# Gate and value projections of two layers as seven block products, with two of a panel's four weight sums on GpSimd

## What is computed

```python
def swiglu(u, w1, w3, w2):
    return (jax.nn.silu(u @ w1) * (u @ w3)) @ w2

for l in range(DEPTH):                                   # DEPTH = 2
    ada = (c_act @ w_ada[l] + b_ada[l])[:, None, :]
    sh1, sc1, g1, sh2, sc2, g2 = jnp.split(ada, 6, axis=-1)
    u = h * (1.0 + sc1) + sh1
    y = mixer(u, ...)
    h = layer_norm(DN_ALPHA * h + g1 * y, ln1_g[l], ln1_b[l])
    u = h * (1.0 + sc2) + sh2
    y = swiglu(u, w1[l], w3[l], w2[l])
    h = layer_norm(DN_ALPHA * h + g2 * y, ln2_g[l], ln2_b[l])
```

## Time and profile before

| | us |
|---|---|
| median of 3 runs | 2424.16 |
| lowest and highest run | 2416.7 and 2425.68 |
| the profiled execution | 2416.46 |
| its span, first to last instruction | 2414.7 |

### The profile page before, as it was taken

The page is one execution under the profiler, slowest core; times in us unless marked ns, Lnnn a source line. Parts: engine busy times, 40 slices in busy tenths (PEclk is TensorE's granted clock), DMA queues, the critical chain, the costliest instruction groups (busy, mean ns, idle before and its releaser), DMA issues.

```text
span 2414.7 us, 27153 instructions
## 1 busy us (share of the span) xinstructions
PE 2324.4 (96%) x10982; PEld 1835.2 (76%) x10982; DVE 1253.5 (52%) x2360; ACT 494.2 (20%) x1048; POOL 62.6 (3%) x93
## 2 busy tenths in 40 slices
PE   7999999999999999999999999999999999888998
PEld 5888587788768876868887655588888874567987
DVE  5764311432746432125777266775566455556666
ACT  1222320100011223101011355312200032432200
POOL 0100000000000000000000000000000000000000
PEclk9999999999999999999999999999999999999999
DMA  9853433674475333336874101433333245134442
GB/s 392 321 210 106 156 122 126 233 289 166 175 283 196 134 110 145 124 136 249 305 288 166 35 36 36 148 113 134 121 123 140 79 141 187 74 113 170 161 158 79
DMA packets 163499, 391.18 MB, mean 162 GB/s; under 512 B 6448, under 2 KB 10928, under 8 KB 160560
## 3 DMA queue, kind: packets, MB, share of 16 engines
q1 hardware_dynamic: 136736, 285.03, 32.7%
q0 software_dynamic: 24080, 93.69, 10.6%
q10 hardware_dynamic: 2560, 10.72, 1.2%
HBM read 388.37 MB, written 1.05 MB: 161 GB/s over the span
## 4 chain that ended last, share of the span: by engine, by line
PE 91%; DVE 4%; ACT 2%; DMA 1%; issue 1%; DVEq 0%; SPq 0%; ACTq 0%
PE bank L503 89%; DVE arena L1946 2%; PE bank L501 2%; ACT arena L1335 2%; DVE arena L1952 1%; DMA arena<-in_w_ada 1%; ACT arena L1338 1%; DVE arena L1949 0%; DMA arena<-in_x 0%; DVE arena L2827 0%; ACT L1335 0%; DVE arena L2084 0%; DVE arena L2011 0%; DVE arena L2015 0%; DVE arena L2859 0%
## 5 line engine op out<-in xcount | busy, mean ns | idle before, releaser
L503 PE MATMUL bank<-arena 128*128 128x256 f32 (+6 forms) x10494 | 2267.1, 384 | 47.4 <-ACT arena L1335 15.2
L503 PEld LDWEIGHTS bank<-arena 128*128 128x128 f32 (+2 forms) x10494 | 1777.0, 189 | 524.7 <-issue 283.7
L1946 DVE TENSOR_TENSOR arena<-arena 128x1024 f32<-128x1024 f32 (+9 forms) x497 | 374.8, 767 | 231.0 <-PE bank L503 194.3
L1952 DVE SCALAR_TENSOR_TENSOR arena<-arena 128x1028 f32<-128x1028 f32 (+6 forms) x367 | 304.5, 845 | 101.6 <-DMA arena<-in_w_ada 66.7
L1335 ACT ACTIVATE arena<-arena 128x512 f32<-128x512 f32 (+5 forms) x386 | 196.7, 533 | 709.8 <-DVE arena L1946 357.5
L1946 DVE TENSOR_TENSOR arena<-bank,arena 128x512 f32<-128x512 f32 (+3 forms) x123 | 83.7, 690 | 471.4 <-PE bank L503 445.0
L1338 ACT ACTIVATE arena<-bank 128x512 f32<-128x512 f32 (+1 forms) x227 | 127.4, 596 | 707.8 <-PE bank L503 667.2
L1335 ACT ACTIVATE arena<-bank 128x256 f32<-128x256 f32 (+2 forms) x99 | 41.3, 438 | 400.3 <-PE bank L503 399.6
L1946 DVE TENSOR_TENSOR arena<-arena,bank 128x256 f32<-128x256 f32 (+2 forms) x172 | 85.4, 521 | 64.6 <-PE bank L503 59.8
L2970 POOL DMA_DIRECT2D arena<-in_w_ada x88 | 61.8, 702 | 2141.4 <-DVEq L1961 2135.4
L1952 DVE SCALAR_TENSOR_TENSOR arena<-bank,arena 128x254 f32<-128x254 f32 (+2 forms) x184 | 78.0, 468 | 51.4 <-PE bank L501 35.2
(11 more groups left out here) (31 smaller groups left out, 132.0 us busy)
## 6 DMA issues: line engine op xcount, KB each, us to landing
arena<-in_w_ada POOLq DMA_DIRECT2D x88, 1028.0 KB, 6.1
arena<-in_w_in SPq DMA_DIRECT2D x84, 1024.0 KB, 7.1
arena<-in_w SPq DMA_DIRECT2D x56, 1024.0 KB, 7.3
arena<-in_w_mlp_in SPq DMA_DIRECT2D x32, 1024.0 KB, 6.4
arena<-in_w_mlp_out SPq DMA_DIRECT2D x32, 1024.0 KB, 6.5
arena<-in_w_gla SPq DMA_DIRECT2D x12, 1024.0 KB, 7.3
arena<-in_w_ada SPq DMA_DIRECT2D x16, 514.0 KB, 19.2
arena<-in_w_a SPq DMA_DIRECT2D x8, 1024.0 KB, 6.9
```

Source lines behind the costliest of these rows:

```text
L503: ins = nc.tensor.matmul(out, lhsT, rhs, start=start, stop=stop)
L1946: return V.tensor_tensor(out, x, y, op)
L1952: return V.scalar_tensor_tensor(out=out, in0=x, scalar=s, in1=y, op0=op0, op1=op1, **kw)
```

## The change

1. The ten full panels (five of w1, five of w3, in turn, `UP`) become seven products each: 56 matmuls with 128 moving columns in place of 32 with 256. Tile 10 of both stays as it was. Products 1 and 2 of the first two panels need only the first half of the tokens and stand where the half tiles stood.
2. Of a panel's four weight sums POOL makes `w5` (into `down_sum`) and `w7` (in place), in `weight_sums`, DVE makes `w6` and `w3`. POOL's sums for a panel wait for product 5 of the panel before and for that panel's `w6`.
3. DVE makes four token sums once per layer and, per panel, seven sums of product tiles (128 by 256). ACT copies product 1 and applies the Silu to the four finished blocks of a W1 panel in SBUF; DVE multiplies with W3 once per panel pair (128 by 1024).
4. The twelve ada turns of each layer leave the projections: they stand in the mix (`beside_mix`), one behind each of WA 0, WA 1 and WB 0, five behind WB 1, one behind each of WA 2, WA 3, WB 2 and WB 3. Of the eight further turns of layer 1, four stand behind up panels 2, 4, 6 and 8, and four at the start of the attention stage.
5. The affine step of the residual rows (four sums of 128 by 1024) is spread behind up panels 2 to 5; on ACT some parameter DMAs are issued later.

```diff
-                w1, w3, tiles = panel(), panel(), {}
-                half_tiles(("W1 0", "W3 0"), (w1, w3), 0, 0, tiles)
+                def up(name, p, order):
+                    q = quarters(first_of[l, "w1"] + 2 * UP.index((name, p)))
+                    ops = {1: (q[0], up_x[0]), 2: (q[1], up_x[2]), 4: (q[3], up_sums[4]), 5: (down_sum, up_sums[5]),
+                           7: (q[2], up_sums[7]), 6: (q[0], up_sums[6]), 3: (q[1], up_x[3])}
+                    for i in order:
+                        key = f"{name} {p} {i}"
+                        ps = open_tile(key)
+                        if i in (4, 5, 6, 7):
+                            pe.wait_ge(dve_done, DV.at(f"U x{i}"))
+                        if i in (6, 3):
+                            pe.wait_ge(dve_done, DV.at(f"{name} {p} w{i}"))
+                        if i in (5, 7):
+                            pe.wait_ge(up_sums_made, made(l, UP.index((name, p)), i))
...
+                w1, w3 = panel(), panel()
+                drained("U 0 0")
+                drained("U 0 1")
+                for name in ("W1", "W3"):
+                    up(name, 0, FIRST_ORDER[:2])
                 pe.wait_ge(dve_done, DV.at("ln1 1"))
                 tile_transposes("U", 1)
-                half_tiles(("W1 0", "W3 0"), (w1, w3), 0, 1, tiles)
...
+                for name, w in (("W1", w1), ("W3", w3)):
+                    up(name, 0, FIRST_ORDER[2:])
+                    release(w)
+                for name, p in UP[2:]:
+                    w = panel()
+                    up(name, p, ORDER)
+                    release(w)
...
+            def up_panel(at):
+                name, p = UP[at]
+                key = f"{name} {p}"
...
+                dve.wait_ge(up_sums_made, made(l, at, 7))
+                panel_sums(key, n, 6, f"{key} 1", down_sum)
+                panel_sums(key, n, 3, f"{key} 2", down_sum)
+                first_sum(key, c, read)
+                for _ in product_sums(key, c, read):
+                    pass
+                if name == "W3":
+                    dve.wait_ge(act_done, AC.at(f"gated {p}"))
...
+                    tt_(x, x, up_out("W1", p), ALU.mult).then_inc(dve_done, DV.step(f"up {p}"))
...
                         tt_(MIX[:, 2 * j:2 * j + 2, :].rearrange("p a b -> p (a b)"), ps[:, :], sg[:, 2 * n, :], ALU.mult).then_inc(
                             dve_done, DV.drained(f"WA {j}"))
+                        beside_mix(1)
...
                         tt_(x, x, sg[:, 2 * n + 1, :], ALU.add).then_inc(dve_done, DV.step(f"mix {j}"))
+                        beside_mix({0: 1, 1: 5, 2: 1, 3: 1}[j])
...
+                token_sums("U", up_x, [up_sums[i] for i in (5, 6, 4)], False, up_sums[7])
+                for at in range(len(UP)):
+                    up_panel(at)
+                    if 2 <= at < 6:
+                        affine_step("U", at - 2)
+                    if l == DEPTH - 1 and at in (2, 4, 6, 8):
+                        ada_turn(7 + at // 2, [("ada", 1), ("adax", 2)])
...
+            for q in range(12, 16):
+                ada_turn(q, [("ada", 1), ("adax", 2)])
...
+            def weight_sums(l, at):
+                n = first_of[l, "w1"] + 2 * at
+                a11, a12, a21, a22 = quarters(n)
+                for m in (n, n + 1):
+                    pool.wait_ge(panel_in[m % RING], 16 * (m // RING + 1))
+                if at:
+                    name, p = UP[at - 1]
+                    pool.wait_ge(pe_of[f"layer {l}"], PE.of(f"layer {l}", f"{name} {p} 5 full"))
+                    pool.wait_ge(dve_of[f"layer {l}"], DV.of(f"layer {l}", f"{name} {p} w6"))
...
+                nc.gpsimd.tensor_tensor(down_sum, a21, a22, ALU.add).then_inc(up_sums_made, 1)
+                pool.wait_ge(up_sums_made, made(l, at, 5))
+                nc.gpsimd.tensor_tensor(a21, a11, a21, ALU.subtract).then_inc(up_sums_made, 1)
```

245 lines of the change are left out of this document (144 added, 101 removed).

## The result

The changed kernel takes 2425.4 us (median of 20 runs, 2419.9 to 2432.1), the kernel before 2422.2 beside it (20 runs): a ratio of 1.0016, with a 95% interval of 1.0009 to 1.0024. The forecast was 2418, which is 6.3 us less than the median of the kernel before that was then known; against the 2422.2 measured beside the change, 6.3 us less is 2415.9, and the change lies 9.5 us above it. The time lies in the stated range, and it is no change by the bound of 0.5%, but it moved a little the other way, although the seven products do on PE what was forecast of them. The profiled execution took 2421.2, its span 2418.9, 4.2 longer than before.

What follows compares the result with a forecast made beforehand. PE, busy 96% of the span, was taken to bound the kernel. 7.6 + 9.7 - 0.5 - 5.5 - 5.0 = 6.3 us less gave 2418 us against the median, with a range of 2402 to 2432.

Steps and rivals of the forecast that it cites:

- A panel of 12.50 us: Up projections: a panel as seven products takes 12.50 us in place of 13.87, read from the GLA stage's mlp in.
- Restart 2.2 us later: Behind the second transposes, layer 0: PE restarts at 447.4 us, where it was 445.17.
- Bank 3: At W3 0's product 5: PE stands 4.6 us until DVE, in its turn, frees the bank of W3 0's product 2.
- The stretch: From PE's restart to the last value tile: 138.5 us, 7.6 us less in layer 0 and 9.7 less in layer 1.
- DVE's and GpSimd's room in the steady part: Steady panels: DVE under 8 of 12.50 us, 0.6 to spare in layer 1; GpSimd sums under 5.6 us cost nothing.
- Rival C: Steady panels: POOL's sum takes over 5.6 us and PE waits for product 6; 2430 to 2470 us, chance 0.12.
- The rule 2X + 1.3: Steady panels: two POOL sums of X us plus 1.3 must stay under 12.50 us, so X under 5.6 costs nothing.
- The mix in layer 1: Ahead of WO in layer 1: the turns make WB 3's step 5.5 us late, with fetched data already there.
- rival D: In the mix: turns' fetches crowd it and the turn behind WB 1 ends late; 2421 to 2424 us, chance 0.07.
- The clock: Behind three longer PE waits, W3 0 in each layer and WO in layer 1: 1.67 us each, 5.0 us, range 0 to 8.4.
- Attention's start: Start of the attention stage: four turns, 20.4 us and about 2 for slots, hide in 23.84 us idle, 1.4 to spare.
- Rival B: W3 of W1 0 and layer 1's tight places: POOL and DVE disturb each other, up to 8 us; 2420 to 2428, chance 0.15.

Runs made afterwards that it cites:

- early_sum: The change with the DVE sum that reads bank 3 moved ahead of W1 0's five other sums, w6 and w3: 2411.4 us, ratio 0.9954 to the kernel before.
- sums_dve: The change with the weight sums w5 and w7 on DVE in place of GpSimd: 2439.5 us, ratio 1.0072 to the kernel before.
- pool_x5: The change with each panel's first weight sum made four times by GpSimd, five sums in place of two: 2490.8 us, ratio 1.0285 to the kernel before.
- the second profile: The changed kernel itself, nothing altered, profiled a second time: 2417.6 us.
- before_seam: The kernel before, with PE's first half tiles of W1 0 and W3 0 waiting for both blocks of U 0: 2426.4 us, ratio 1.0022.
- wo_turns: The change with the turns behind WA 3 and WB 2 moved behind WO's first two tiles: 2416.4 us, ratio 0.9978 to the kernel before.

## Where the prediction held and where it failed

- **A panel of 12.50 us: right.** PE is busy and at full clock in a steady panel, and GpSimd's sums in layer 0 come every 12.51 us. The GLA stage was a good model.
- **Restart 2.2 us later: right** (2.2 in both layers). The order of PE's waits gave it.
- **Bank 3: right.** 4.62 and 4.61 us for 4.6. `early_sum` shows that it was this one instruction's place in DVE's queue. The profile puts the wait down to "issue" and not to DVE, as the prediction had said it would; the cause was found from the order of the queue.
- **The stretch: right without the clock.** With the later restart counted in, layer 0 gained 4.4 us up to the last value tile (6.6 - 2.2) and layer 1 6.4 (8.6 - 2.2). From 461.87 it took 125.7 us where 122.8 were reckoned, which is 2.9 for the clock; in layer 1 it is 3.0. Without these the gains are 7.3 and 9.4, for 7.6 and 9.7.
- **DVE's and GpSimd's room in the steady part: right.** X, the length of one of GpSimd's sums, is 2.35 us, or 3.4 where a sum of DVE holds it up. Layer 1's tight places held with some 0.3 us to spare behind panels 2 and 4, for the 0.6 reckoned: in `sums_dve` 2.45 us more of DVE's work made PE wait 2.11. Rival C did not come, and its point of decision lies lower than 5.8. The rule 2X + 1.3, put for five sums, gives a pitch of 13.7 us, and `pool_x5` has 15.4 and 16.2 in turn: it leaves out that DVE's w3 and gating product stand in GpSimd's way.
- **The mix in layer 1: the term of 5.5 us was mis-sized, it measured 9.2.** The step that failed is "The data are there: a slot's fetch takes 6.1 us". DVE waited 2.2 us for a fetch ahead of the turn behind WA 2, and 2.2 ahead of that behind WB 2 (DVE's timeline of the changed kernel):

```profile
1044.01 1.23 DVE L2009 SCALAR_TENSOR_TENSOR junk<-arena 128x1028 bf16<-128x1028 f32 x1 [2.17 <-DMA arena<-in_w_ada]
1058.97 1.23 DVE L2009 SCALAR_TENSOR_TENSOR junk<-arena 128x1028 bf16<-128x1028 f32 x1 [2.21 <-DMA arena<-in_w_ada]
...
1064.23 0.69 DVE L2003 TENSOR_TENSOR arena<-bank,arena 128x512 f32<-128x512 f32 x1 [0.21 <-DVE arena L2009]
```

  The seven fetches issued from 1020 to 1070 us landed after 5.2 to 9.5 us, with a median of 8.1, where 6.1 was the median of the whole kernel before. The kernel before has no fetch of `w_ada` in that stretch; beside the seven new ones the mix's own panels of `w_out` also landed later (median 7.6 for 6.2 us), while the queues moved 277 GB/s where it was 147. So the fetches crowding each other, rival D's first half, is the likely cause, though no run moved the fetches alone. The delay varies: WO is 6.3 us late in the second profile, and 9.6 to 10.2 in the three other kernels that keep these turns in the mix. Layer 0's 0.5 was right.
- **The clock: the term of 5.0 us was mis-sized, and it is the larger part of the miss.** The step that failed is the price of one stall, 1.67 us, taken from one row. Behind the three waits it measured 2.9 + 3.0 + 2.9 = 8.8 us, over the term's upper end of 8.4. That row's wait is 3 us long, the new ones are 4.6 to 10.7. The waits of 2.8 and 2.3 us were left out; they cost no clock in this profile, but they did in five of the eight that have them. The profiles differ by 10.7 us of clock in all, for 3.3 us were lost at 720 to 732 us and 0.2 at 661, and 1.6 at 1327 us came back. These 1.9 us can't be put down to the change: the place at 720 us is low in `before_seam` too, and the kernel before was profiled in an execution with a mean clock of 0.992, where its others have 0.988 to 0.992.
- **Attention's start: right.** The four turns there end at 1359.0, and DVE's next piece of work comes 2.5 us later, for 1.4 reckoned. The low clock of before at 1327 us is not there, which is luck as far as the runs show: `early_sum` and `sums_dve`, with the same four turns, have it.
- **Rival B: its mechanism is true, its price was not.** GpSimd and DVE do meet at the places that it names, w3 of W1 0 in both layers and the tight places of layer 1 (3.38 and 3.37 us for 2.35, and one sum of DVE of 2.23). That is also a sign of being wrong that the prediction had set, DVE sums over 1.23 us while GpSimd works. But PE waited nowhere for it, so it cost nothing where 8 us were reckoned: W3 0's wait is 4.62 us in spite of the clash. In layer 0's steady part the two work in different halves of the panel. A further clash comes at a place that rival B did not name: GpSimd's first sums of each layer, beside WO's residual steps. There PE waited for nothing until `wo_turns` filled DVE's room.

The sum, redone: 7.3 + 9.4 - 0.5 - 9.2 - 10.7 = -3.7, and 0.4 us that no term holds, with the rounding, make the 4.2 measured. From a gain of 6.3 to a loss of 3.7 it is 10.0 us: 3.7 for the mix, 3.8 for the clock behind the three waits, 1.9 for the clock elsewhere, and 0.6 in the two stretches. The path was read rightly, each stall came where it was forecast; what the stalls cost was not. That the time still lies in the range is owed to its width.

## What to carry to other kernels

Here the faster products brought nothing while a later bank, sum or turn stood in one engine's queue ahead of what PE needed next. So list, for each wait of PE, what stands in front of the instruction that ends it, and move that. A wait of PE also cost clock on top of its length: 2.9 or 3.0 us behind each of the change's three long waits, and 1.6 to 2.9 us behind the pairs of 2.8 and 2.3 us in 9 places of 16. Take such a price from more than one row, and from waits as long as the one in question. Two engines that hide behind a third need room that their own clashes don't use up: moving work within a full stretch moved the wait, and taking a piece out of it removed it.
